# A two-layer transformer block and a third block on one core: norms between stages by token block, and an order of up panels

## The chip, the cores and the metric

One core of one Trainium2 chip runs the whole program. The metric is the device time of one execution in microseconds, the median of several runs; lower is better. Engines of the core: TensorE (PE; its weight loads are shown as PEld), VectorE (DVE), ScalarE (ACT), GpSimd (POOL), and SyncE (SP), which here only issues the DMA transfers.

## The reference

256 tokens of width 1024. Two layers (`hybrid_layer`) run one after the other, then a second block of another kind that this change touches only through its feed-forward. One layer is:

```python
shift1, scale1, gate1, shift2, scale2, gate2 = jnp.split(mod[:, None, :], 6, axis=-1)
h = rms_norm(x, norm1) * (1.0 + scale1) + shift1
proj = h @ w_in                       # 1816 columns: pool, queries, keys and values, gates
mix = jnp.concatenate([y_pool, y_nsa], axis=-1) @ w_out
x = x + gate1 * mix
h2 = rms_norm(x, norm2) * (1.0 + scale2) + shift2
ff = jnp.square(jax.nn.relu(h2 @ w_ff1)) @ w_ff2      # 1024 -> 4096 -> 1024
x = x + gate2 * ff
```

with `mod = silu(c) @ w_mod + b_mod` (6144 columns per layer) and `rms_norm(x, g) = x * rsqrt(mean(x * x) + eps) * g`.

## The kernel before

**Numbers.** Every float32 weight and activation is split in two parts of type fp32r: a rounded `hi` and a rest `lo`. A product is three matmuls, hi x hi, hi x lo and lo x hi (`mm3`, lines 433 to 437). `act2` holds `act_hi` and `act_lo` side by side, so in the up matmuls one instruction of 512 columns does hi x (hi and lo) for all 256 tokens (line 803) and one of 256 columns lo x hi (line 804).

**Weights** come in panels of 128 x 2048 (1 MB) through a ring of six. ScalarE copies a panel to `w_hi`, one of four slots (`split_hi`, line 425), VectorE writes the rest into the ring in place (`split_lo`, line 430), TensorE uses it and frees the slot (`pe_used`). A layer has 44 panels: 8 for the input projections, 4 for the output projection (two pool, two attention: `L_POOL`, `L_ATT`), and 16 up and 16 down panels of the feed-forward (`L_FF` = 12 on).

**Modulation** (`mod`) is computed on VectorE: a unit of `w_mod`, 1 MB, is multiplied by silu(c) and summed (`dve_mod`, line 1196, two instructions per unit). In layer 0, units 8 to 19 are turns 0 to 11 of the attention stage; in layer 1, units 12 to 21 are turns 0 to 9. They are loaded into two buffers in turn by SyncE (`gate_mod` in `sp_layer`): a unit's load waits until the unit two before it is summed.

**Order of the work.** Each engine runs a list written out by hand, and engines wait for each other's semaphores. All queues are in order, so an instruction that waits holds up all that stand behind it on its engine.

**Out projection to feed-forward.** `pe_out` puts the tokens' quarters (block of 128 tokens, half of the columns) into banks 0 to 3. For each quarter VectorE multiplies by the gate row and adds to x (`dve_update`, lines 1215 and 1217); ScalarE squares and sums it (`act_stats`, line 946) and after two quarters has 1/rms of the token block (line 954). VectorE scales the block (`dve_scaled`, line 1224), TensorE transposes it into banks 4 to 7 (`pe_features`, line 585), and per 128 features VectorE (even ones, line 1233) and ScalarE (odd ones, line 981) apply scale and shift for all 256 tokens, ScalarE rounds to `act_hi` and VectorE subtracts (line 1242, `act_ready`). The first up panel (`up_head`, lines 785 and 786) takes the features as they come.

**Feed-forward** (`pe_ff`). Up and down panels take turns, each up one step ahead. Behind an up panel ScalarE and VectorE build the square of the relu and split it (`ff_hi`, line 1155, and `ff_lo`, line 1497, `ff_ready`); a down panel waits for it. The last down panel goes by quarters, so that quarter after quarter of x can be updated.

**Between the layers** the same norm is done, with nothing for TensorE to do beside it: `pe_features`, then `pe_head` of the next layer's first panel. After layer 1, x itself is transposed for the second block, without a norm.

Of the kernel before, what the change touches and what calls it, by code (L numbers as in the profile page):

```python
# [14 lines left out]
P = 128  # L15
# [82 lines left out]
def build(nc, a, out, layers=DEPTH):  # L98
# [8 lines left out]
    with ctx:  # L107
# [141 lines left out]
        hb = [arena[:, y_at + i * T:y_at + (i + 1) * T] for i in range(6)]  # L249
        ybuf = [area(2 * T, 2, T) for _ in range(3)]  # L250
# [115 lines left out]
        def sp_layer(sp, l, ahead):  # L366
# [25 lines left out]
            gate_mod(9)  # L392
            load(sp, m, 14)
            load(sp, m, 15)
            gate_mod(10)
            gate_mod(11)
# [163 lines left out]

        def pe_out(pe, l, m, k, steps=(0, 8)):
# [26 lines left out]

        def pe_gate_row(pe, l, late, h, o):
# [7 lines left out]
        def pe_layer(pe, l, ahead):  # L597
            m = 11 * l

            def arrive(kc):  # L600
                pe.wait_ge(act_ready, 16 * l + max(kc + 1, 2))
# [164 lines left out]
            pe_used(pe, pe_out(pe, l, m, L_ATT + 1, (4, 8)))  # L766
            pe_features(pe, xn, y_ready, 8 * l + 4)
            pe_ff(pe, l, m, lambda kc: pe.wait_ge(act_ready, 16 * l + KC + kc + 1), 16 * l, L_FF)
            if ahead:
                pe_features(pe, xn, y_ready, 8 * l + 8)  # L770
            else:
                pe_features(pe, x, x_ready, 8 * l + 4)

        def pe_ff(pe, l, m, arrive, j0, k0, second=False):


            def up_head(mm, k, jn):

                pe.wait_ge(lo_done, 4 * mm + k + 1)
                wh, wl = w_hi[slot(k)], w_lo(mm, k)  # L780
                for kc in range(KC):
                    arrive(kc)
                    for c in range(2):
                        s = kc * 256 + c * P
                        nc.tensor.matmul(bank[c][:, :], wh[:, s:s + P], act2[:, kc, :, :], start=kc == 0, stop=False, skip_group_check=True)  # L785
                        last = nc.tensor.matmul(bank[c][:, 0:T], wl[:, s:s + P], act_hi[:, kc, :], start=False, stop=kc == KC - 1,
                                                skip_group_check=True)
                        if c == 0 and kc == KC - 1:
                            last.then_inc(ff_full, 1)
                pe_used(pe, last)  # L790
# [457 lines left out]
        def dve_layer(dve, l, link, ahead):  # L1248
# [76 lines left out]
            if l == 0:  # L1325
                split_lo(dve, m, 2)
# [1168 lines left out]
```

## Time and profile before

| | us |
|---|---|
| median of 3 runs | 1243.28 (1242.53 to 1245.27) |
| the profiled execution | 1243.92 |
| its span, first to last instruction | 1242.1 |
| TensorE busy | 1158.9 |
| VectorE busy | 916.0 |
| ScalarE busy | 622.1 |
| mean granted TensorE clock | 0.981 of full speed |

Matmuls are pipelined: a duration in the profile is longer than the time to the start of the next, so the pace is read from the starts. An entry in square brackets at the end of a timeline row is the time that the engine was idle before the instruction, and what released it.

### The profile page before, as it was taken

The page shows a single profiled execution, that of the slowest core. Times are in us where ns is not written, and L with a number is a line of the kernel's source. Part 1 is how long each engine was busy: PE and PEld are TensorE (multiplying, and loading weights), DVE is VectorE, ACT ScalarE, POOL GpSimd, SP SyncE. Part 2 cuts the span into 40 slices and gives each one's busy share as a digit, 9 for nine tenths or more (in the row PEclk, how much of TensorE's full clock was granted, in tenths as well). Part 3 has the DMA queues.
Part 4 walks back from the last instruction along what each step waited for, and adds up shares of the span by engine and source line. Part 5 has one row for each costly group of instructions (what it writes and reads, how often), then busy time and mean ns, then how long its engine had stood idle before and what let it go on. Part 6 is the DMA issues. An engine that isn't in the chain of part 4 may idle for free.

```text
span 1242.1 us, 18002 instructions
## 1 busy us (share of the span) xinstructions
PE 1158.9 (93%) x7130; PEld 1012.3 (81%) x7130; DVE 916.0 (74%) x1192; ACT 622.1 (50%) x851; POOL 58.5 (5%) x61
## 2 busy tenths in 40 slices
PE   1999979999979998999999998999889998999996
PEld 1978858888869787888888997888779997888885
DVE  6889789888767978856567369887984858656555
ACT  3763254444455525544444434568995634444441
POOL 1016000000000430000000000000000000000000
PEclk9999979999989999999999999999999999999998
DMA  9935557868756336555555533346864564555540
GB/s 380 379 128 214 201 188 277 307 244 315 265 205 237 136 103 249 200 177 199 185 186 195 176 135 131 104 154 218 288 223 136 177 231 168 170 177 196 188 150 34
DMA packets 44054, 249.27 MB, mean 201 GB/s; under 512 B 4352, under 2 KB 12672, under 8 KB 15952
## 3 DMA queue, kind: packets, MB, share of 16 engines
q1 hardware_dynamic: 43568, 246.19, 55.1%
q0 software_dynamic: 416, 2.11, 0.4%
q8 instruction: 49, 0.80, 0.3%
q14 instruction: 21, 0.17, 0.0%
HBM read 247.17 MB, written 1.11 MB: 200 GB/s over the span
## 4 chain that ended last, share of the span: by engine, by line
PE 77%; DVE 11%; ACT 5%; DMA 3%; issue 2%; SPq 0%; POOL 0%; DVEq 0%; ACTq 0%; POOLq 0%
PE bank L435 15%; PE bank L436 15%; PE bank L437 15%; PE bank L803 14%; PE bank L804 7%; PE bank L882 2%; DMA raw<-in_panels 2%; DVE ring_w L430 2%; DVE arena L2126 2%; PE bank L923 1%; ACT mixf L1947 1%; PE bank L785 1%; ACT mixf L1948 1%; PE bank L1739 1%; DMA arena<-in_modw 1%
## 5 line engine op out<-in xcount | busy, mean ns | idle before, releaser
L430 DVE TENSOR_TENSOR ring_w<-raw,w_hi 128x2048 fp32r<-128x2048 f32 x170 | 390.5, 2301 | 151.3 <-ACT w_hi L425 150.9
L425 ACT ACTIVATE w_hi<-raw 128x2048 fp32r<-128x2048 f32 x170 | 324.3, 1911 | 159.3 <-PE bank L437 144.6
L803 PE MATMUL bank<-act,w_hi 128*128 128x512 f32 x736 | 262.2, 399 | 0.2 <-DVE act L2263 0.2
L435 PE MATMUL bank<-act,w_hi 128*128 128x256 f32 x792 | 231.9, 293 | 3.6 <-ACT arena L1980 2.0
L436 PE MATMUL bank<-act,w_hi 128*128 128x256 f32 x792 | 226.0, 285 | 0.0
L437 PE MATMUL bank<-act,ring_w 128*128 128x256 f32 x792 | 225.9, 285 | 0.0
L804 PE MATMUL bank<-act,ring_w 128*128 128x256 f32 x736 | 206.6, 281 | 0.0
L803 PEld LDWEIGHTS bank<-act,w_hi 128*128 128x128 f32 x736 | 138.5, 188 | 34.4 <-issue 0.6
L435 PEld LDWEIGHTS bank<-act,w_hi 128*128 128x128 f32 x792 | 153.9, 194 | 12.2 <-issue 9.5
L436 PEld LDWEIGHTS bank<-act,w_hi 128*128 128x128 f32 x792 | 153.9, 194 | 0.1
L437 PEld LDWEIGHTS bank<-act,ring_w 128*128 128x128 f32 x792 | 153.8, 194 | 0.0
L435 PE MATMUL bank<-w_hi,ff_hi 128*128 128x512 f32 x384 | 149.9, 390 | 0.0
L436 PE MATMUL bank<-ring_w,ff_hi 128*128 128x512 f32 x384 | 149.9, 390 | 0.0
L437 PE MATMUL bank<-w_hi,ff_lo 128*128 128x512 f32 x384 | 149.4, 389 | 0.0
L804 PEld LDWEIGHTS bank<-act,ring_w 128*128 128x128 f32 x736 | 139.2, 189 | 1.6
L1148 ACT ACTIVATE arena<-bank 128x256 f32<-128x256 f32 x96 | 36.8, 385 | 160.9 <-PE bank L804 151.5
L1196 DVE CUSTOM_DVE_ANT_0 arena<-arena,crow 128x1024 f32<-128x1024 f32 x88 | 105.9, 1243 | 12.3 <-DMA arena<-in_modw 11.9
L1490 DVE TENSOR_TENSOR arena<-bank,arena 128x256 f32<-128x256 f32 x96 | 39.8, 421 | 64.6 <-ACT arena L1148 64.5
L435 PEld LDWEIGHTS bank<-w_hi,ff_hi 128*128 128x128 f32 x384 | 72.1, 188 | 15.9
L437 PEld LDWEIGHTS bank<-w_hi,ff_lo 128*128 128x128 f32 x384 | 72.1, 188 | 15.4
L436 PEld LDWEIGHTS bank<-ring_w,ff_hi 128*128 128x128 f32 x384 | 72.1, 188 | 13.3
L2126 DVE SCALAR_TENSOR_TENSOR arena<-arena 128x256 f32<-128x256 f32 x96 | 39.1, 479 | 9.7 <-ACT arena L1897 9.7
(349 smaller groups left out, 1652.9 us busy)
## 6 DMA issues: line engine op xcount, KB each, us to landing
raw<-in_panels SPq DMA_DIRECT2D x170, 1024.0 KB, 4.9
arena<-in_modw SPq DMA_DIRECT2D x44, 1024.0 KB, 7.2
mixf<-dscr SPq DMA_DIRECT2D x8, 512.0 KB, 4.9
arena<-dscr SPq DMA_DIRECT2D x8, 512.0 KB, 4.9
mixf<-in_modw SPq DMA_DIRECT2D x2, 1024.0 KB, 16.0
act_flat<-in_modw SPq DMA_DIRECT2D x2, 1024.0 KB, 20.0
mixf<-dscr SPq DMA_DIRECT2D x8, 256.0 KB, 5.9
arena<-dscr SPq DMA_DIRECT2D x8, 256.0 KB, 6.2
```

The source lines that it names most:

```text
L425: nc.scalar.activation(w_hi[slot(k)][:, :], w_raw(m, k), ACT.Copy).then_inc(hi_done, 1)
L430: nc.vector.tensor_tensor(w_lo(m, k), w_raw(m, k), w_hi[slot(k)][:, :].bitcast(F32), ALU.subtract).then_inc(lo_done, 1)
L435: nc.tensor.matmul(o, wh, xh, start=start, stop=False, skip_group_check=skip)
L436: nc.tensor.matmul(o, wh, xl, start=False, stop=False, skip_group_check=skip)
L437: return nc.tensor.matmul(o, wl, xh, start=False, stop=stop, skip_group_check=skip)
L803: nc.tensor.matmul(bank[4 + c][:, :], wh[:, s:s + P], act2[:, kc, :, :], start=kc == 0, stop=False)
L804: last = nc.tensor.matmul(bank[4 + c][:, 0:T], wl[:, s:s + P], act_hi[:, kc, :], start=False, stop=kc == KC - 1)
L882: mm = lambda o, w, x, first=False, last=False: nc.tensor.matmul(o, w, x, start=first, stop=last, skip_group_check=True)
L1148: nc.scalar.activation(fr[par][:, c * T:(c + 1) * T], up_bank(at, c, final)[:, T:2 * T], ACT.Copy).then_inc(ff_cross, 1)
L1196: last = nc.vector.tensor_tensor_reduce(o, o, crow[:, :], 1.0, 0.0, ALU.mult, ALU.add, sums[:, col + b:col + b + 1])
L1490: nc.vector.tensor_tensor(fr[par][:, c * T:(c + 1) * T], up_bank(at, c, final)[:, 0:T], fr[par][:, c * T:(c + 1) * T], ALU.add).then_inc(f ...
L2126: ins = nc.vector.scalar_tensor_tensor(xb[:, b, :], src, w, xb[:, b, :], ALU.mult, ALU.add)
```

## The change

Four edits. (1) The norm before the feed-forward and the norm between the layers go by two blocks of 128 tokens: ScalarE now scales a block, TensorE transposes it into banks 6 and 7, VectorE and ScalarE take four features each, and rounding and subtraction go by four features (512 columns) at a time. (2) The first two up panels of layers 0 and 1 run per token block: first panel on block 0, half of the second panel on block 0, the transposes of block 1, the other half, then both panels on block 1. (3) In layers 0 and 1 the last two down panels run by quarters. (4) The modulation sums stand one place or more earlier in VectorE's list, and their loads ahead of panels 14 and 15 in SyncE's. Besides, `up` issues a column half's eight wide matmuls and then its eight narrow ones, in all three feed-forwards.

```diff
+        def block_feature(kc):
+            return bank[6 + kc % 2][:, kc // 2 * P:(kc // 2 + 1) * P]
...
+            gate_mod(10)
+            gate_mod(11)
...
+        def pe_quarter(m, k, xh, xl, final, n):
+            wh, wl = w_hi[slot(k)], w_lo(m, k)
+            tt, h = n // 2, n % 2
+            for kk in range(2):
+                ts, s = slice(kk * T + tt * P, kk * T + (tt + 1) * P), slice(kk * D + 512 * h, kk * D + 512 * (h + 1))
+                last = mm3(bank[n][:, :], xh[:, ts], xl[:, ts], wh[:, s], wl[:, s], False, final and kk == 1, skip=True)
+            return last
...
+        def pe_block_features(pe, q, tt):
+            pe.wait_ge(y_ready, 4 * q + 2 * tt + 2)
+            for kc in (0, 2, 4, 6, 1, 3, 5, 7):
+                last = nc.tensor.transpose(block_feature(kc), xn[:, tt, kc * P:(kc + 1) * P], ident)
+                if kc >= 6:
+                    last.then_inc(xt_full, 1)
...
-                pe.wait_ge(act_ready, 16 * l + max(kc + 1, 2))
+                pe.wait_ge(act_ready, 16 * l + (6 + 2 * (kc // 4) if l else max(kc + 1, 2)))
...
-            pe_used(pe, pe_out(pe, l, m, L_ATT + 1, (4, 8)))
-            pe_features(pe, xn, y_ready, 8 * l + 4)
-            pe_ff(pe, l, m, lambda kc: pe.wait_ge(act_ready, 16 * l + KC + kc + 1), 16 * l, L_FF)
+            pe_out(pe, l, m, L_ATT + 1, (4, 6))
+            pe_block_features(pe, 2 * l + 1, 0)
+            pe_used(pe, pe_out(pe, l, m, L_ATT + 1, (6, 8)))
+            first, second = bank[0:2], bank[4:6]
+            pe_up_block(pe, l, m, L_FF, first, 0, range(KC))
+            pe_up_block(pe, l, m, L_FF + 1, second, 0, range(4))
+            pe_block_features(pe, 2 * l + 1, 1)
+            pe_up_block(pe, l, m, L_FF + 1, second, 0, range(4, KC))
+            pe_up_rest(pe, l, m, L_FF, first)
+            pe_up_rest(pe, l, m, L_FF + 1, second)
+            pe_ff(pe, l, m, None, 16 * l, L_FF)
             if ahead:
-                pe_features(pe, xn, y_ready, 8 * l + 8)
+                pe_block_features(pe, 2 * l + 2, 0)
+                pe_block_features(pe, 2 * l + 2, 1)
...
+        def pe_up_one(m, k, o, c, kc, tt):
+            wh, wl = w_hi[slot(k)], w_lo(m, k)
+            s, ts = kc * 256 + c * P, slice(tt * P, (tt + 1) * P)
+            both = o[c][:, :].rearrange("p (b t) -> p b t", b=2)[:, :, ts]
+            nc.tensor.matmul(both, wh[:, s:s + P], act2[:, kc, :, ts], start=kc == 0, stop=False, skip_group_check=True)
+            return nc.tensor.matmul(o[c][:, ts], wl[:, s:s + P], act_hi[:, kc, ts], start=False, stop=kc == KC - 1, skip_group_check=True)
+        def pe_up_block(pe, l, m, k, o, tt, kcs):
+            pe.wait_ge(lo_done, 4 * m + k + 1)
+            for kc in kcs:
+                pe.wait_ge(act_ready, 16 * l + KC + 4 * tt + 2 + 2 * (kc // 4))
+                for c in range(2):
+                    pe_up_one(m, k, o, c, kc, tt)
+        def pe_up_rest(pe, l, m, k, o):
+            for c in range(2):
+                for kc in range(KC):
+                    pe.wait_ge(act_ready, 16 * l + KC + 6 + 2 * (kc // 4))
+                    last = pe_up_one(m, k, o, c, kc, 1)
+                if c == 0:
+                    last.then_inc(ff_full, 1)
+            pe_used(pe, last)
...
                         nc.tensor.matmul(bank[4 + c][:, :], wh[:, s:s + P], act2[:, kc, :, :], start=kc == 0, stop=False)
+                    for kc in range(KC):
+                        s = kc * 256 + c * P
                         last = nc.tensor.matmul(bank[4 + c][:, 0:T], wl[:, s:s + P], act_hi[:, kc, :], start=False, stop=kc == KC - 1)
...
+                a = (e, k0 + 2, ff_hi[:, 0, :], ff_lo[:, 0, :], False)
+                b = (e, k0 + 3, ff_hi[:, 1, :], ff_lo[:, 1, :], True)
+                pe.wait_ge(ff_ready, 2 + j0 + FF_STEPS - 1)
+                pe.wait_ge(lo_done, 4 * e + k0 + 3)
+                for n in (0, 1, 2):
+                    pe_quarter(*a, n)
+                pe.wait_ge(ff_ready, 2 + j0 + FF_STEPS)
+                pe.wait_ge(lo_done, 4 * e + k0 + 4)
+                pe_quarter(*b, 0).then_inc(rows_done, 1)
+                pe_quarter(*b, 1).then_inc(rows_done, 1)
+                pe_used(pe, pe_quarter(*a, 3))
+                pe_quarter(*b, 2).then_inc(rows_done, 1)
+                pe_used(pe, pe_quarter(*b, 3))
...
+        def act_scaled(act, q, tt):
+            act.wait_ge(rs_done, 2 * q + tt + 1)
+            for h in range(2):
+                cols = slice(512 * h, 512 * (h + 1))
+                nc.scalar.activation(xn[:, tt, cols], x[:, tt, cols], ACT.Copy, scale=rs[:, tt:tt + 1]).then_inc(y_ready, 1)
+        def act_block(act, q, tt, g0, shift):
+            act.wait_ge(gcol_ready, q + 1)
+            act.wait_ge(xt_full, 4 * q + 2 * tt + 2)
+            if tt:
+                act.wait_ge(act_ready, 8 * q + 4)
+            for j in range(2):
+                for kc in (4 * j + 1, 4 * j + 3):
+                    last = nc.scalar.activation(hn[:, kc, :], block_feature(kc), ACT.Identity, bias=modc[:, shift + kc:shift + kc + 1],
+                                                scale=gcol[:, g0 + kc:g0 + kc + 1])
+                last.then_inc(h_done, 1)
+                act.wait_ge(t_done, 4 * q + 2 * tt + j + 1)
+                act.wait_ge(h_done, 4 * q + 2 * tt + j + 1)
+                nc.scalar.activation(act_hi[:, 4 * j:4 * j + 4, tt * P:(tt + 1) * P], hn[:, 4 * j:4 * j + 4, :], ACT.Copy).then_inc(act_his, 2)
...
-            for n in range(3):
-                act_stats(act, 2 * l + 1, n)
+            q = 2 * l + 1
+            act_stats(act, q, 0)
+            act_stats(act, q, 1)
+            act_scaled(act, q, 0)
+            act_block(act, q, 0, KC, 24)
+            act_stats(act, q, 2)
+            act_stats(act, q, 3)
+            act_scaled(act, q, 1)
+            act_block(act, q, 1, KC, 24)
             split_hi(act, m, 14)
-            act_stats(act, 2 * l + 1, 3)
-            act_norm(act, l, 2 * l + 1, 24, KC)
             act_ff(act, l, m, L_FF, 16 * l)
...
+                q = 2 * l + 2
+                for tt in range(TT):
+                    act_stats(act, q, 2 * tt)
+                    act_stats(act, q, 2 * tt + 1)
+                    act_scaled(act, q, tt)
+                    act_block(act, q, tt, 0, 0)
...
+        def dve_block(dve, q, tt, g0, shift):
+            dve.wait_ge(gcol_ready, q + 1)
+            dve.wait_ge(xt_full, 4 * q + 2 * tt + 1)
+            for kc in (0, 2, 4, 6):
+                last = nc.vector.tensor_scalar(hn[:, kc, :], block_feature(kc), gcol[:, g0 + kc:g0 + kc + 1], modc[:, shift + kc:shift + kc + 1],
+                                               ALU.mult, ALU.add)
+                if kc % 4:
+                    last.then_inc(t_done, 1)
+            for j in range(2):
+                v, ts = slice(4 * j, 4 * j + 4), slice(tt * P, (tt + 1) * P)
+                dve.wait_ge(act_his, 8 * q + 4 * tt + 2 * j + 2)
+                nc.vector.tensor_tensor(act_lo[:, v, ts], hn[:, v, :], act_hi[:, v, ts].bitcast(F32), ALU.subtract).then_inc(act_ready, 2)
...
+            mod(3)
...
             mixed(1)
+            mod(8)
             for g in range(4):
                 dve.wait_ge(pool_his, 4 * l + g // 2 * 2 + 2)
@@ -1417,15 +1520,15 @@
                 if g % 2:
                     last.then_inc(gfree[g // 2], 1)
             weigh(4)
+            mod(9)
             weigh(5)
             split_lo(dve, m, 11)
             weigh(6)
-            mod(7)
+            mod(10)
             mixed(2)
             weigh(7)
+            mod(11)
             mixed(3)
...
+            split_lo(dve, m, 13)
             update(0)
-            mod(10)
-            update(1)
-            mod(11)
             dve_modc(dve, modc_ready, 4 * l + 3, 24, lc[:, LC_BM + 8:LC_BM + 24], MOD_PANELS * l + (22 if l else 20))
             nc.vector.scalar_tensor_tensor(gcol[:, KC:2 * KC], modc[:, 32:40], 1.0, lc[:, LC_N2:LC_N2 + KC], ALU.add, ALU.mult).then_inc(gcol_ready, 1)
+            update(1)
             update(2)
-            dve_scaled(dve, 2 * l + 1, 0)
+            dve_block(dve, 2 * l + 1, 0, KC, 24)
             update(3)
-            dve_scaled(dve, 2 * l + 1, 1)
-            dve_norm(dve, 2 * l + 1, KC, 24)
-            split_lo(dve, m, 13)
+            dve_block(dve, 2 * l + 1, 1, KC, 24)
             split_lo(dve, m, 14)
...
-                    dve_scaled(dve, 2 * l + 2, n - 2)
+                    dve_block(dve, 2 * l + 2, n - 2, 0, 0)
+            if ahead:
+                split_lo(dve, m + 11, 2)
```

The first `mod(3)` line stands between the compression and `rotated(0)`; further down, the `mod(3)` to `mod(6)` of before become `mod(4)` to `mod(7)` in their places.

## Rows read from the trace of the kernel before

**Rows 1.** The page: busy us (share of the span) of each engine, xinstructions

```profile
PE 1158.9 (93%) x7130; PEld 1012.3 (81%) x7130; DVE 916.0 (74%) x1192; ACT 622.1 (50%) x851; POOL 58.5 (5%) x61
```

**Rows 2.** Timeline of TensorE, layer 1, projection to feed-forward: start, duration, engine, line, op

```profile
482.96 1.03 PE L585 MATMUL bank<-cst,arena 128*128 128x128 f32 x8
...
488.72 0.77 PE L785 MATMUL bank<-act,w_hi 128*128 128x512 f32 x1 [1.14 <-DVE act L1242]
...
495.81 0.40 PE L803 MATMUL bank<-act,w_hi 128*128 128x512 f32 x1
...
501.45 0.40 PE L435 MATMUL bank<-w_hi,ff_hi 128*128 128x512 f32 x1
...
506.92 0.39 PE L803 MATMUL bank<-act,w_hi 128*128 128x512 f32 x1
```

**Rows 3.** Timeline of TensorE, streams of 256 columns (layer 1) and of 60 (layer 0)

```profile
365.77 0.28 PE L435 MATMUL bank<-act,w_hi 128*128 128x256 f32 x1
...
371.88 0.28 PE L435 MATMUL bank<-act,w_hi 128*128 128x256 f32 x1
...
62.08 0.28 PE L435 MATMUL bank<-ff_hi,w_hi 128*128 128x60 f32 x1
...
63.08 0.28 PE L435 MATMUL bank<-ff_hi,w_hi 128*128 128x60 f32 x1
```

**Rows 4.** Timelines of VectorE and TensorE, layer 0, rotation and pool copies

```profile
68.21 0.69 DVE L1271 TENSOR_TENSOR arena<-bank,cst 128x512 f32<-128x512 f32 x1 [3.33 <-PE bank L613]
...
119.42 1.22 DVE L1196 CUSTOM_DVE_ANT_0 arena<-arena,crow 128x1024 f32<-128x1024 f32 x1
...
123.06 0.42 DVE L1322 TENSOR_TENSOR mix_lo<-bank,mix_hi 128x256 fp32r<-128x256 f32 x1 [1.28 <-ACT mix_hi L1066]
...
124.12 1.74 DVE L1415 SCALAR_TENSOR_TENSOR mix_lo<-bank,lc,mix_hi 128x256 fp32r<-128x256 f32 x4 [0.63 <-ACT mix_hi L1118]
...
125.05 0.48 PE L919 MATMUL bank<-vca,act_flat 32*128 32x130 f32 x2 [0.54 <-DVE mix_lo L1415]
```

**Rows 5.** Timelines of VectorE and TensorE, layer 0, projection to feed-forward

```profile
153.53 1.23 DVE L1196 CUSTOM_DVE_ANT_0 arena<-arena,crow 128x1024 f32<-128x1024 f32 x1 [2.41 <-DMA arena<-in_modw]
...
155.39 0.39 PE L437 MATMUL bank<-w_hi,mix_lo 128*128 128x512 f32 x1
...
168.58 0.76 PE L785 MATMUL bank<-act,w_hi 128*128 128x512 f32 x1 [0.72 <-DVE act L1242]
...
182.52 0.40 PE L435 MATMUL bank<-w_hi,ff_hi 128*128 128x512 f32 x1
```

**Rows 6.** Timelines of ScalarE and VectorE, layer 1: rounding of panel 13, first ff_lo

```profile
472.33 1.92 ACT L425 ACTIVATE w_hi<-raw 128x2048 fp32r<-128x2048 f32 x1 [2.44 <-PE bank L437]
...
500.44 0.69 DVE L1497 TENSOR_TENSOR ff_lo<-arena,ff_hi 128x512 fp32r<-128x512 f32 x1
```

**Rows 7.** Timeline of ScalarE: root of a block (layer 1), scaled copies (start of the program)

```profile
479.82 0.63 ACT L946 ACTIVATE arena<-x 128x512 f32<-128x512 f32 x1 [0.28 <-DVE x L1217]
...
480.91 0.20 ACT L954 ACTIVATE rs<-sq_log 128x1 f32<-128x1 f32 x1
...
9.85 1.34 ACT L2382 ACTIVATE arena<-x,rs 128x512 f32<-128x512 f32 x2
```

**Rows 8.** Timelines of VectorE and TensorE, layer 0 to layer 1

```profile
346.69 2.29 DVE L430 TENSOR_TENSOR ring_w<-raw,w_hi 128x2048 fp32r<-128x2048 f32 x1
...
348.89 0.68 DVE L1215 TENSOR_TENSOR arena<-bank,arena 128x512 f32<-128x512 f32 x1
...
350.22 0.68 DVE L1215 TENSOR_TENSOR arena<-bank,arena 128x512 f32<-128x512 f32 x1
...
349.51 0.39 PE L437 MATMUL bank<-w_hi,ff_lo 128*128 128x512 f32 x1
...
360.10 0.55 PE L435 MATMUL bank<-act,w_hi 128*128 128x256 f32 x1 [1.05 <-DVE act L1242]
...
365.36 0.33 PE L435 MATMUL bank<-act,w_hi 128*128 128x256 f32 x1
```

More of the change, by code:

```diff
@@ L771, in pe_layer @@
             else:
                 pe_features(pe, x, x_ready, 8 * l + 4)
-        def pe_ff(pe, l, m, arrive, j0, k0, second=False):
[L777 to L790, printed above, removed]
+        def pe_up_one(m, k, o, c, kc, tt):
[4 more added lines that the diff above has]
+            return nc.tensor.matmul(o[c][:, ts], wl[:, s:s + P], act_hi[:, kc, ts], start=False, stop=kc == KC - 1, skip_group_check=True)
@@ L814, in pe_ff @@
                 up(m, k0, j0, 0, arrive)
-            else:
-                up_head(m, k0, j0)
-            up(m, k0 + 1, j0 + 1, 1, waits=second)
+                up(m, k0 + 1, j0 + 1, 1)
             down(m, k0 + 2, j0, 0, True, False)
@@ L832, in pe_ff @@
             up(e, k0 + 1, j0 + FF_STEPS - 1, 1)
-            down(e, k0 + 2, j0 + FF_STEPS - 2, 0, False, False)
-            down(e, k0 + 3, j0 + FF_STEPS - 1, 1, False, True)
+            if second:
+                down(e, k0 + 2, j0 + FF_STEPS - 2, 0, False, False)
+                down(e, k0 + 3, j0 + FF_STEPS - 1, 1, False, True)
+            else:
+                a = (e, k0 + 2, ff_hi[:, 0, :], ff_lo[:, 0, :], False)
[11 more added lines that the diff above has]
+                pe_used(pe, pe_quarter(*b, 3))
         pair_of = lambda ap: ap.rearrange("p (b s) -> p b s", b=2)
@@ L1217, in dve_update @@
             nc.vector.tensor_tensor(x[:, tt, cols], x[:, tt, cols], xn[:, tt, cols], ALU.add).then_inc(x_ready, 1)
-        def dve_scaled(dve, q, tt):
-            dve.wait_ge(rs_done, 2 * q + tt + 1)
-            for h in range(2):
-                cols = slice(512 * h, 512 * (h + 1))
-                nc.vector.tensor_scalar(xn[:, tt, cols], x[:, tt, cols], rs[:, tt:tt + 1], None, ALU.mult).then_inc(y_ready, 1)
+        def dve_block(dve, q, tt, g0, shift):
[10 more added lines that the diff above has]
+                nc.vector.tensor_tensor(act_lo[:, v, ts], hn[:, v, :], act_hi[:, v, ts].bitcast(F32), ALU.subtract).then_inc(act_ready, 2)
         def dve_norm(dve, q, g0, shift):
@@ L1395, in dve_layer @@
             stack(1)
-            mod(3)
+            mod(4)
             split_lo(dve, m, 8)
-            mod(4)
+            mod(5)
             split_lo(dve, m, 9)
@@ L1405, in dve_layer @@
                 dve_modc(dve, modc_ready, 4 * l + 2, 16, lc[:, LC_BM:LC_BM + 8], 12)
-            mod(5)
+            mod(6)
             weigh(2)
@@ L1409, in dve_layer @@
             mixed(0)
-            mod(6)
+            mod(7)
             mixed(1)
+            mod(8)
             for g in range(4):
@@ L1422, in dve_layer @@
             weigh(6)
-            mod(7)
+            mod(10)
             mixed(2)
             weigh(7)
+            mod(11)
             mixed(3)
-            mod(8)
-            mod(9)
             def update(n):
```

11 lines of the change are left out of this document (4 added, 7 removed).

## The prediction

> **What bounds the kernel now.** I read the page first: TensorE is busy for 93% of the span [rows 1]. So a change pays where TensorE stands still or runs slowly, and costs where it gets more matmuls. Next the timeline of TensorE alone, where the start-to-start step counts (the durations overlap). In the feed-forward an up panel (32 matmuls) takes 495.81 to 501.45, 5.64 us, and a down panel (24) 501.45 to 506.92, 5.47 us [rows 2]; all panels of the three feed-forwards that I measured repeat these two numbers within 0.03 us, without a gap. The engine is short of work at the stage borders, and these I read last, engine by engine: out projection to feed-forward in both layers (part 3), and layer 0 to layer 1 (part 4).
>
> **1. The up panel's new order.** `up` now issues 8 matmuls of 512 columns and then 8 of 256, where it alternated; 44 panels go through it (14 in each layer, 16 in the last feed-forward; 2 per layer now go through the block helpers). All are on TensorE's path. Alternating, a pair costs 5.64/16 = 0.3525 us. A stream of 512 columns alone costs 5.47/24 = 0.228 [rows 2], one of 256 alone (371.88-365.77)/51 = 0.120 [rows 3]: 0.348 a pair, 0.08 us less per panel, 44 times: **-3.5 us**. No row shows grouped weights of both kinds, so the bounds are 0 (nothing is saved by the order) and -5.3 (half as much again). I take -3.5, since both streams are rows.
> The Trainium skill, page "TensorE: Matmul & The Clock Gate", section "Back-to-back issue gap", gives the gap of a single matmul as N/2.4 + 2.5 ns, 109 and 216 ns here, whatever stands beside it; by it the order changes nothing. The rows are above it by 11 ns each, and the pair by 28 ns.
>
> **2. Modulation sums moved forward.** One sum is two multiply-reduces of 1.22 us that overlap a little, 2.3 us in all [rows 4]. The one now ahead of the rotation lies in an idle stretch of VectorE of 3.3 us [rows 4]: nothing, unless its unit lands over 1 us late. The one between the first two pairs of weighings takes the place of another: nothing. But `mod(8)` now stands between `mixed(1)` and the four pool copies. VectorE is free there only from about 123.4 to 124.1, then the copies start, and TensorE waits for them (idle 0.54 with the copy as releaser) [rows 4]. The sum ends at 123.4+2.3 = 125.7, 1.6 us after the copies began before; TensorE gets its banks that much later. Both layers: **+3.2 us**. Bounds: +2.4 (a shorter start) to +5 (the sum's own DMA late). The sums behind weighings 4, 6 and 7 lie where VectorE waits for TensorE or ScalarE anyway, and delay at most its last mix copy, which TensorE needs only with the fourth matmul group of the attention part: nothing. On SP, units 18 and 19 now go ahead of panels 14 and 15. A unit is issued when the sum two before it is done, and these sums now end before the panel whose slot the load of panel 14 needs: no queue delay; if they came late, panel 14 would, and with it a split that has some 20 us in hand.
>
> **3. Out projection to feed-forward.** The length counts from the end of the projection to the first down panel. Before: layer 1 482.96 to 501.45, 18.5 us [rows 2]; layer 0 155.62 to 182.52, 26.9 us, longer because VectorE waits 2.4 us for a sum's DMA and then does sums before it updates x [rows 5].
> After, in layer 1's times: panel 13's rounding ends on ScalarE at 474.2 [rows 6]; VectorE subtracts it (2.2), updates 0 and 1 (1.33 each [rows 8]), so x's second quarter is there at 479.5. ScalarE needs 1.3 for the root and 1.35 for the two scaled copies that it takes over [rows 7]: xn at 482.2. TensorE has done all but 6 matmuls at 481.6, waits 0.6, transposes (1.0 [rows 2]), does the 6 and is at 484.7. Behind the transposes a block needs: 1.1 for them, ScalarE's two 128-column pieces and one 512-wide copy (1.45, estimated from the 1.35 for two such copies), VectorE's subtraction 0.7 [rows 6]: first half at 3.3 us, second half at 4.6 us. So the first up panel starts at 485.6, 3.1 us earlier than 488.72.
> But the block matmuls cost more. A pair is 256+128 columns. The 256 costs 0.12; for 128 no row is at hand, but 60 columns cost (63.08-62.08)/9 = 0.111 [rows 3], so a narrow matmul is not under that: 0.23 a pair, twice, against 0.3525. Bounds for the 128: 0.06 (half of the 256) to 0.21 (as slow as at half clock). I take 0.11. The two panels have 64 such pairs, 14.7 us, against 11.3.
> The last update of x is queued behind block 0's subtraction (487), the stats of block 1 behind that: x at 488.2, xn at 490.9, block 1's first half at 494.3, its second at 495.7. TensorE has done its three portions of block 0 and one of block 1 at 493.8, waits about 0.5 twice, ends the first panel's second column half at 498.4 and the second panel at 502.0. Then what is late is the first ff half: from the first panel's end to its `ff_lo` 495.81 to 501.13, 5.3 us [rows 2, 6], was hidden behind a whole up panel of 5.64; now behind 3.6. The first down panel starts at 498.4+5.4 = 503.8.
> So the length is 20.8 in both layers (layer 0's sums no longer decide): layer 1 **+2.4**, layer 0 **-6.1**. Bounds: 17.4 (narrow matmuls at 0.06, no ff wait) and 25 a layer.
>
> **4. Layer 0 to layer 1.** TensorE ends at 349.74 and starts layer 1 at 360.10 [rows 8]. The quarters bring x's rows earlier, but VectorE is busy until 346.69 anyway; it gains the 2.2 us of the weight subtraction that stood there [rows 8]. Three updates end at 350.75, the root is ready at 350.75 too, scaled copies 352.1, transposes, block 0 done on VectorE at 356.7. Only then comes the last update (358.1), root 359.4, scaled copies 360.8, transposes at half clock (2 us), first half of block 1 at about 365.1; and the layer's head needs both blocks. No matmul fills this. Before, the four updates ran one behind the other. **+5.0 us**. Bounds +2.5 and +7. Half the clock for the head is paid in both (25 matmuls from 360.10 to 365.36 take 0.21 each against 0.12 [rows 3, 8]), 2.2 us, give or take 1.
>
> **5. Before the second block** the last quarter ends at the same time, and its update is the last before the head: 0. Bounds -0.7 and +1.
>
> **Sum:** -3.5 + 3.2 + 2.4 - 6.1 + 5.0 = **+1.0 us**, on the profiled execution's 1243.92 (span 1242.1 and 1.8 around it). This execution is 0.6 above the median of the runs, 1243.28; the forecast is that median plus 1.0, **1244.3 us**.
>
> **Rivals.**
> A. *The pipelining pays in full, 0.29.* TensorE's block matmuls run at 0.09, the ff half comes in time behind the second panel, and the order of `up` gives 5.3. For it: the first down panel's wait in my sum is only 1.8 us and rests on four estimated pieces. Against it: the 60-column row. Layers -1.8 each, `up` -1.8 more: 1.0-5.4 = -4.4, **1238.9 us**.
> B. *Slower: the order of `up` gives nothing, 0.21.* Place: 44 panels. Price: my -3.5 goes. It decides as soon as a grouped pair costs 0.3525. Everything else stands at +4.5: **1247.8 us**. For it: a pair's excess over its two streams is 0.005 us, so small that it may belong to something else in the panel than the order. That is also where the page's rule leads.
> C. *Slower: TensorE's clock falls at the block border, 0.08.* Its waits of 0.6 to 1.8 us there follow one another; before, a 2.5 us idle had it at half speed for the head in layer 1. Up to 2.5 us per layer: **1249 us**.
> D. *The blocks do nothing, 0.04:* the head waits as before and the narrow matmuls' 3.4 us are pure cost. Layer 1 18.5+3.4, and layer 0 the same, 5.0 below its 26.9: with the other parts +3.1, **1246.4 us**.
> My own forecast: 0.38.
>
> **How the numbers follow.** A measurement here tells 0.2% (2.5 us) from no change. Faster: A 0.27 and 0.03 of my own forecast's spread, 0.30. Slower: B 0.17, C and D 0.12, 0.04 of my own, 0.33. Same: 0.37. Since the sides nearly balance, the likeliest case's own range is 1241 to 1247.5; the range to hold 8 in 10 is 1238.5 to 1249.5.
>
> **What would show it.** Right: the granted clock still falls between the layers, and layer 1's first panel starts some 15 us after layer 0's last down matmul (10.4 before); TensorE idles about 2 us before the pool copies' consumer in both layers; up panels take 5.56; the first down panel waits for `ff_lo` and starts about 21 us after the projection's end in both layers. Wrong: 128-column matmuls at 0.06 or at 0.2; up panels at 5.64; a head of layer 1 before 362; the pool copies not moved.

## The result and the profile after

The change makes the kernel slower: 1255.69 us median of 8 runs (1248.42 to 1267.90) against 1243.75 (1242.53 to 1246.08); the ratio of comparable runs is 1.0072, 95% interval 1.0046 to 1.0099. Forecast were 1244.3 us and a range to 1249.5. The ratios leave out a run that is over 1.5% above the fastest of its kernel: here the profiled execution, the slowest of the eight, 1267.90 us, span 1266.1. Its page:

```profile
span 1266.1 us, 18288 instructions
...
PE 1177.9 (93%) x7258; PEld 1034.0 (82%) x7258; DVE 912.6 (72%) x1180; ACT 633.0 (50%) x863; POOL 58.6 (5%) x61
...
PEclk9999799999969988999999999899999999899999
```

TensorE's share is the same 93% as before [rows 1], so the page's first line says nothing. PEclk (the granted clock in 40 equal slices, in tenths of full speed) has a 7 in its fifth digit and 8s in its fifteenth and sixteenth, where before has 9s. I then took the start of each stage's first matmul from TensorE's timeline; the table has the lengths in us of the profiled executions, those of the experiments (below) beside them. "Order" is the new order in the up panels, "sums" the moved modulation sums.

| stage on TensorE | before | after | sums | sums, ninth behind the copies | the same + order | + mid blocks | + border blocks, quarters | all, ninth sum behind |
|---|---|---|---|---|---|---|---|---|
| first matmul stream to layer 0's projection | 103.9 | 113.3 | 105.7 | 104.2 | 104.5 | 104.7 | 103.9 | 104.8 |
| layer 0: projection's start to first down panel | 40.6 | 35.5 | 32.9 | 32.4 | 33.4 | 35.5 | 33.2 | 35.5 |
| last two down panels of layer 0 to layer 1's head | 21.3 | 28.1 | 21.3 | 21.3 | 21.3 | 21.3 | 27.4 | 27.2 |
| layer 1: head to projection | 109.1 | 118.6 | 110.3 | 108.6 | 108.2 | 108.6 | 108.3 | 109.4 |
| layer 1: projection's start to first down panel | 32.2 | 35.7 | 33.0 | 33.4 | 33.1 | 35.5 | 33.2 | 37.3 |
| the same feed-forward from there | 156.3 | 155.4 | 156.3 | 156.3 | 155.3 | 157.0 | 155.3 | 155.4 |

Before to after the spans differ by 24.0 us: +9.4 and +9.5 in the two attention stages, +6.8 between the layers, +3.5 in layer 1's border, -5.2 in layer 0's, -0.9, -0.9 and -1.1 in the feed-forwards; 2.8 are the program's start (0.5) and the second block (2.3), which the change does not touch. Most of the 2.3 is a fall of the clock too: behind a wait of 1.83 us, from 932.4 to 936.0 at a granted clock of 0.54, where before has the same wait of 1.83 us and no fall. The two big terms are not in my sum. What they are is seen in the stretch behind the pool copies. First after, by windows (stretch, its length, busy us and count of PE, PEld, DVE, ACT and POOL, granted clock PEclk, DMA share, GB/s):

```profile
127.22:144.66 17.44, 17.44 (x57) 13.91 (x57) 10.55 (x20) 0.61 (x1) 0.00 (x0) 0.51 0.36 122
151.81:187.27 35.46, 31.25 (x206) 27.75 (x205) 23.95 (x36) 22.31 (x42) 0.00 (x0) 1.00 0.53 191
342.65:370.72 28.07, 15.01 (x67) 12.00 (x65) 16.53 (x29) 14.88 (x33) 0.61 (x1) 0.73 0.55 203
...
464.68:482.00 17.32, 17.32 (x57) 13.79 (x57) 9.74 (x19) 0.61 (x1) 0.00 (x0) 0.51 0.00 1
489.30:525.02 35.72, 31.24 (x207) 27.74 (x205) 22.53 (x32) 22.30 (x42) 0.59 (x1) 1.00 0.56 201
```

The same windows of before:

```profile
125.05:134.73 9.68, 9.68 (x57) 7.73 (x57) 6.49 (x14) 2.19 (x2) 0.00 (x0) 1.00 0.09 36
141.89:182.52 40.63, 31.76 (x143) 26.32 (x141) 32.90 (x52) 17.98 (x36) 0.00 (x0) 0.83 0.61 236
338.83:360.10 21.27, 14.13 (x66) 11.27 (x65) 17.59 (x28) 11.03 (x23) 0.61 (x1) 0.89 0.71 266
469.23:501.45 32.22, 28.59 (x142) 24.00 (x141) 28.24 (x44) 18.00 (x36) 0.59 (x1) 0.95 0.64 243
```

The 57 matmuls from the first one behind the pool copies took 9.7 us at full clock before and take 17.4 us after, TensorE busy all the time, at a granted clock of 0.51: the level of 1.2 GHz. That is 7.8 us, in each layer. The wait right ahead of the fall stands in TensorE's timeline of after, both layers:

```profile
127.22 0.80 PE L979 MATMUL bank<-vca,act_flat 32*128 32x130 f32 x2 [2.11 <-DVE mix_lo L1518]
...
464.68 0.48 PE L979 MATMUL bank<-vca,act_flat 32*128 32x130 f32 x2 [2.11 <-DVE mix_lo L1518]
```

and VectorE's timeline of after, layer 0, has the reason of the wait:

```profile
123.67 0.42 DVE L1423 TENSOR_TENSOR mix_lo<-bank,mix_hi 128x256 fp32r<-128x256 f32 x1 [1.29 <-ACT mix_hi L1150]
124.00 1.22 DVE L1289 CUSTOM_DVE_ANT_0 arena<-arena,crow 128x1024 f32<-128x1024 f32 x1
...
125.15 1.22 DVE L1289 CUSTOM_DVE_ANT_0 arena<-arena,crow 128x1024 f32<-128x1024 f32 x1
...
126.29 1.66 DVE L1518 SCALAR_TENSOR_TENSOR mix_lo<-bank,lc,mix_hi 128x256 fp32r<-128x256 f32 x4
```

The ninth sum starts at 124.00 and the copies behind it only at 126.29, and TensorE stands 2.11 us instead of 0.54 [rows 4]: 1.57 us a layer, as forecast (1.6). The fall of the clock behind it was not.

The up panels went as forecast. TensorE's timeline of after, one panel of layer 1 in four groups of 8:

```profile
530.60 1.98 PE L848 MATMUL bank<-act,w_hi 128*128 128x512 f32 x8
532.41 1.12 PE L851 MATMUL bank<-act,ring_w 128*128 128x256 f32 x8
533.36 2.00 PE L848 MATMUL bank<-act,w_hi 128*128 128x512 f32 x8
535.20 1.12 PE L851 MATMUL bank<-act,ring_w 128*128 128x256 f32 x8
536.15 0.40 PE L440 MATMUL bank<-w_hi,ff_hi 128*128 128x512 f32 x1
```

530.60 to 536.15 is 5.55 us against 5.64 [rows 2]; a wide matmul steps 0.226, a narrow one 0.119.

### The profile page after: what moved, and what is told of

Same layout as the page of the kernel before. It is cut to its first block, busy times and chain, and to the rows that moved or that the text cites. A ratio compares the mean times of both kernels' runs of the same rounds, so it can differ in the third digit from the quotient of the medians.

```text
span 1266.1 us, 18288 instructions
## 1 busy us (share of the span) xinstructions
PE 1177.9 (93%) x7258; PEld 1034.0 (82%) x7258; DVE 912.6 (72%) x1180; ACT 633.0 (50%) x863; POOL 58.6 (5%) x61
## 3 DMA queue, kind: packets, MB, share of 16 engines
q0 software_dynamic: 416, 2.11, 0.5%
## 4 chain that ended last, share of the span: by engine, by line
PE 53%; DVE 10%; ACT 5%; issue 2%; POOL 0%; DVEq 0%; ACTq 0%
PE bank L440 11%; PE bank L441 11%; PE bank L442 11%; PE bank L848 9%; PE bank L851 5%; DVE ring_w L435 2%; DVE arena L2227 2%; PE bank L942 1%; ACT mixf L2048 1%; PE bank L983 1%; ACT w_hi L430 1%; ACT mixf L2049 1%; PE bank L1840 1%; PE bank L1894 1%; PE bank L813 0%
## 5 line engine op out<-in xcount | busy, mean ns | idle before, releaser
L435 DVE TENSOR_TENSOR ring_w<-raw,w_hi 128x2048 fp32r<-128x2048 f32 x170 | 390.5, 2300 | 157.5 <-ACT w_hi L430 157.0
L442 PE MATMUL bank<-act,ring_w 128*128 128x256 f32 x792 | 226.1, 285 | 0.0
L848 PE MATMUL bank<-act,w_hi 128*128 128x512 f32 x704 | 177.5, 395 | 0.6 <-DVE act L2364 0.6
L440 PEld LDWEIGHTS bank<-act,w_hi 128*128 128x128 f32 x792 | 154.2, 195 | 14.1 <-issue 11.6
L441 PEld LDWEIGHTS bank<-act,w_hi 128*128 128x128 f32 x792 | 154.2, 195 | 0.1
L442 PEld LDWEIGHTS bank<-act,ring_w 128*128 128x128 f32 x792 | 154.0, 194 | 0.0
L848 PEld LDWEIGHTS bank<-act,w_hi 128*128 128x128 f32 x704 | 130.5, 190 | 26.1 <-issue 0.8
L851 PEld LDWEIGHTS bank<-act,ring_w 128*128 128x128 f32 x704 | 96.9, 192 | 7.0
L851 PE MATMUL bank<-act,ring_w 128*128 128x256 f32 x704 | 99.0, 284 | 0.0
```

What stands on the lines that cost most here:

```text
L435: nc.vector.tensor_tensor(w_lo(m, k), w_raw(m, k), w_hi[slot(k)][:, :].bitcast(F32), ALU.subtract).then_inc(lo_done, 1)
L440: nc.tensor.matmul(o, wh, xh, start=start, stop=False, skip_group_check=skip)
L441: nc.tensor.matmul(o, wh, xl, start=False, stop=False, skip_group_check=skip)
L442: return nc.tensor.matmul(o, wl, xh, start=False, stop=stop, skip_group_check=skip)
L848: nc.tensor.matmul(bank[4 + c][:, :], wh[:, s:s + P], act2[:, kc, :, :], start=kc == 0, stop=False)
L851: last = nc.tensor.matmul(bank[4 + c][:, 0:T], wl[:, s:s + P], act_hi[:, kc, :], start=False, stop=kc == KC - 1)
```

## Experiments

The theory after these rows: the change's own work costs some 4 to 5 us net, and the clock's fall behind the pool copies 7.5 us in each layer and run in which it happens. The eight times of after lie in such steps, and so do their mean granted clocks: three at 1248.4 to 1249.4 (0.985), four at 1255.4 to 1257.2 (0.977 to 0.979), one at 1267.9 (0.968). The rivals: the loss comes from the border between the layers, or the clock falls for a reason of its own. Ratios are to before on the same chip; the interval stands behind. Medians of two kernels come in part from different chips, and their differences are good to about 1 us: before itself has medians of 1243.8, 1244.0 and 1245.6 on the three chips of these runs.

**The ninth sum behind the copies, the rest as after.**

```
             mixed(1)
-            mod(8)
             for g in range(4):   # the four pool copies
             ...
+            mod(8)
             weigh(4)
```

> After, with the ninth modulation sum (mod(8)) behind the four pool copies instead of ahead of them; nothing else. Theory 1 (clock): in the profiled run of after, TensorE stood 2.1 us for the pool copies in each layer and ran at half clock from there for 17 us, so the sum cost 1.6 us plus up to 7.8 us per layer. Then this kernel shows no half clock between 125 and 145 us nor in the same place of layer 1, the second pair of pool matmul groups takes its 9.7 us again, and the median is 1243 to 1247 us. Theory 2 (only the delay of 1.6 us a layer comes from the sum, the clock falls for another reason): 1252.5 us, half clock still there.

Measured 1248.48 us (7 runs, 1245.45 to 1252.76), ratio 1.0039 (1.0021 to 1.0058). The windows behind the copies, layers 0 and 1, and the two borders behind them:

```profile
125.50:135.20 9.70, 9.70 (x58) 7.75 (x58) 9.49 (x19) 2.19 (x2) 0.00 (x0) 1.00 0.58 194
452.93:462.70 9.77, 9.77 (x58) 7.82 (x58) 9.56 (x19) 2.17 (x2) 0.00 (x0) 1.00 0.09 34
333.19:360.42 27.23, 14.16 (x67) 11.29 (x65) 16.53 (x29) 14.88 (x33) 0.61 (x1) 0.76 0.56 209
469.77:507.07 37.30, 32.83 (x206) 29.30 (x204) 22.63 (x32) 22.29 (x42) 0.59 (x1) 0.95 0.53 192
```

The clock stays up, the 58 matmuls take 9.7 us again, and 7.2 us of the median go with one moved sum. By the ratios of the two kernels, 1.0072 and 1.0039, it is 4.1 us, and their intervals overlap; so the clock in the rows shows the effect here, and the pair of kernels below shows it in the times. No run reaches after's usual 1255. The median is 1.5 above my span of 1243 to 1247: the rest costs more than I had it.

**The sums alone, on before.** The edit is the part of the diff that moves `mod(...)` and `gate_mod(...)`.

> Before, with the modulation sums and the loads of their units moved as in the change; no other part. Theory 1 (clock): slower by the delay of 3.2 us and by 0 to 7.8 us per layer, different from run to run: 1247 to 1262 us, with TensorE at half clock behind the pool copies in at least one layer of the profile. Theory 2 (the delay alone): 1247.0 us in every run, no half clock there.

1242.87 us (11 runs), ratio 0.9998 (0.9972 to 1.0025): eight runs at 1239.1 to 1244.0 and three at 1251.6, 1255.9 and 1258.0, where before never exceeded 1248.4 in 24. In the profiled execution TensorE waits 2.11 us in both layers and the clock does not fall:

```profile
127.41:137.10 9.69, 9.69 (x58) 7.73 (x58) 8.59 (x18) 0.62 (x1) 0.00 (x0) 1.00 0.66 217
...
448.26:458.00 9.74, 9.74 (x58) 7.79 (x58) 8.64 (x18) 0.62 (x1) 0.00 (x0) 1.00 0.00 0
```

So a wait of 2.1 us may or may not be followed by the fall, and my demand that it show in this profile was a miss. So was the median: both theories had 1247 us or more. The table has what I had under-read: the sums alone shorten layer 0's border from 40.6 to 32.9 us.

**The same with the ninth sum behind the copies.**

```
             mixed(1)
             for g in range(4):   # the four pool copies
             ...
+            mod(8)
             weigh(4)
+            mod(9)
             weigh(5)
```

> Before, with the modulation sums and their loads moved as in the change, but the ninth sum (mod(8)) behind the pool copies; no other part. Theory 1 (clock): no wait of 2.1 us for the pool copies, so no half clock there in any run, and the runs lie close together; what the moved sums bring remains: with the ninth sum ahead of the copies layer 0's out projection to its first down panel took 32.9 us against 40.6 before. 1243.8 - 7.7 + about 1 in layer 0 and 1 in layer 1: 1238 us, no run above 1244. Theory 2 (the spread of 1239 to 1258 us has nothing to do with the place of this sum): the same median of 1243, and again some runs above 1250.

1237.73 us (7 runs, 1236.34 to 1242.50), ratio 0.9954 (0.9938 to 0.9970). No high runs, 5.1 us below the kernel with that one sum ahead, and the intervals of the two ratios lie apart. Moving the sums is worth 6.3 us, if the ninth keeps off the copies.

**The order of the up panels alone.**

```
                     for kc in range(KC):
                         ... wide matmul
+                    for kc in range(KC):
+                        s = kc * 256 + c * P
                         last = ... narrow matmul
```

> Before, with only the order of the matmuls in the up panels changed (8 wide, then 8 narrow). In after a panel takes 5.56 us instead of 5.64. If that is the order's doing: 44 x 0.08 = 3.5 us less, 1240.2 us, panels of 5.56 us. Rival (the shorter panel has another reason, or the clock gives the gain back): 1243.7 us.

1240.63 us (12 runs), ratio 0.9982 (0.9972 to 0.9992): -3.2 us, panels of 5.56. The gain is the order's.

**Order and sums together (ninth behind the copies).** No blocks, no quarters.

> The same, and the new order in the up panels (8 wide, then 8 narrow): no blocks, no quarters. If the two parts add: 3.5 us less than the kernel with the sums alone, 1234.5 us, better than before and after. If the gains cancel through the clock: 1238 us.

1235.40 us (6 runs), ratio 0.9925 (0.9912 to 0.9938). In medians the order gives -2.3 on top of the sums against -3.2 alone, in ratios -3.6 against -2.2: the parts add as far as these runs can tell. This kernel is the base of the rest, since it leaves out exactly the blocks and the quarters.

**Base plus the blocks between projection and feed-forward.** Edit: the parts of the diff at `pe_block_features(pe, 2 * l + 1, ...)`, `pe_up_block`, `act_block` and `dve_block`.

> The same as the kernel with up order and moved sums, plus the blocks between out projection and feed-forward in both layers; norm between the layers and last down panels as in before. Theory: the blocks cost; layer 0's projection to first down panel took 35.5 us in every kernel with blocks and 32.9 with the sums moved and no blocks, layer 1's 35.5 to 37.3 against 32.2 to 33.0: +2.5 and +3 to +4.5, so 6 to 7 us more than without them, 1241 us. Rival (it is the sums that were kept from working by the blocks' wait on the layer's clock, the blocks themselves pay as my rival A had it): 1.8 us less per layer, 1231 us.

1240.75 us (12 runs), ratio 0.9977 (0.9965 to 0.9989): +5.35 us (6.5 by the ratios). Both borders take 35.5 us at full clock, against 33.4 and 33.1 at a granted clock of 0.90 without blocks. Rival A is out. In this execution the clock falls right behind layer 1's border, which costs the feed-forward 1.6 us (157.0 against 155.4); in the first experiment it fell inside that border, at 0.95 above, 37.3 against 35.5. These are 2 of the 8 block borders in the profiled executions of the four kernels that have them, and the waits ahead of them were short: 1.51 us here, 0.98 and 0.30 us there.

```profile
143.36:178.83 35.47, 31.28 (x207) 27.76 (x205) 24.20 (x36) 22.30 (x42) 0.00 (x0) 1.00 0.53 191
...
464.10:499.56 35.46, 31.26 (x206) 27.74 (x204) 22.54 (x32) 22.29 (x42) 0.59 (x1) 1.00 0.55 201
499.56:656.56 157.00, 157.00 (x792) 134.04 (x793) 99.77 (x95) 70.72 (x71) 0.00 (x0) 0.99 0.54 187
```

**Base plus the blocks between the layers, with quarters.** Edit: the parts of the diff at `2 * l + 2` and `pe_quarter`.

> The same as the kernel with up order and moved sums, plus the blocks between layer 0 and layer 1 and the last down panels by quarters; the norms inside the layers as in before. Theory: from layer 0's last two down panels to layer 1's first matmul 27.2 us instead of 21.3, and the rest unchanged: 5.9 us more than without them, 1240.5 us. Rival (the stretch is long only because the layer's clock had been pushed down by what came before it): 22 to 24 us, 1236 us.

1240.79 us (9 runs), ratio 0.9970 (0.9958 to 0.9982): +5.4 us (5.6 by the ratios), the stretch 27.4 us. The rival is out.

**After with the old norm between the layers, quarters kept.**

> After, with the norm between layer 0 and layer 1 done as in before (one block of 256 tokens, root scaled on VectorE, the weight subtraction ahead of the updates); quarters, mid norms and modulation sums stay as in after. In after, the stretch from layer 0's last down panels to layer 1's first matmul takes 28.1 us against 21.3 before. Theory: that is the two blocks' doing; 5 to 6.8 us less than after, about 1250 us, the stretch back at 21 us. Rival (the quarters or the clock make it long): 1255.7 us, stretch still 26 to 28 us.

1254.95 us (4 runs, 1253.54 to 1258.45), ratio 1.0101 (1.0086 to 1.0116). A miss: the median hardly moved, and the stretch took 23.8 us, not 21. With so few runs, in which the clock falls as it likes, the median can't show 4 us; in the profiled one it fell in layer 0 alone, at the same wait of 2.11 us in both layers:

```profile
127.25:145.00 17.75, 17.75 (x59) 14.06 (x59) 11.19 (x22) 0.61 (x1) 0.00 (x0) 0.52 0.36 120
...
459.86:469.50 9.64, 9.64 (x57) 7.73 (x57) 8.54 (x18) 0.62 (x1) 0.00 (x0) 1.00 0.01 2
```

The 23.8 us asked for a kernel of their own.

**Base plus the quarters alone.**

> The kernel with up order and moved sums (1235.4 us), plus only the last two down panels of the first two feed-forwards by quarters; norms as in before. The kernel that had the quarters under the old norm between the layers took 23.8 us from the last down panels to layer 1's first matmul, against 21.3: the slot of the last but one panel comes free later, ScalarE's rounding of layer 1's first panel and VectorE's subtraction wait for it, and the updates are queued behind that. Theory: 23.8 us again, +2.5 us, 1237.9 us. Rival (it was the half clock of that run, 13.7 us long): 21.3 us, 1235.4 us.

1237.81 us (5 runs), ratio 0.9940 (0.9925 to 0.9954), the stretch 23.8 us: +2.4 us in medians of different chips, 1.9 by the ratios, whose intervals overlap; the 2.5 us show in the stretch. VectorE's timeline between the layers:

```profile
338.18 0.17 DVE L1483 SCALAR_TENSOR_TENSOR gcol<-modc,lc 128x8 f32<-128x8 f32 x1
340.81 2.29 DVE L430 TENSOR_TENSOR ring_w<-raw,w_hi 128x2048 fp32r<-128x2048 f32 x1 [2.46 <-ACT w_hi L425]
343.01 0.68 DVE L1242 TENSOR_TENSOR arena<-bank,arena 128x512 f32<-128x512 f32 x1
```

The subtraction of layer 1's first panel waits 2.46 us for its rounding, as the slot comes free only with the quarter that the last but one panel now does late, and the updates are queued behind it. Before, it did not wait [rows 8]. The quarters bring x's rows earlier, and nothing takes them earlier.

**How long TensorE must stand.** First one of the ninth sum's two reduces ahead of the copies, then both the ninth and the tenth sum.

```
             mixed(1)
+            mod(8, 0)            # first half of the sum; in the other kernel: mod(8), mod(9)
             for g in range(4):
             ...
-            mod(8)
+            mod(8, 1)
```

> The kernel with up order and moved sums, where the ninth sum is split: its first multiply-reduce (1.22 us) ahead of the pool copies, the second behind them. TensorE's idle time there should be about 1.0 us (0.54 without a sum, 2.11 with a whole one). Theory (the clock falls only if TensorE stands long enough there): 0 to 1 us more than 1235.4 us, no half clock behind the pool copies in the profile and no run above 1243. Rival (any delay tips it in some runs): some runs 7 us above the others.

> The kernel with up order and moved sums, with the ninth and tenth sums both ahead of the pool copies; TensorE should stand some 4.4 us there in each layer. Theory: delay of 3.9 us a layer less the 1 us that the later sum cost, and half clock behind the pool copies in both layers in most runs, 7.5 us each: 1235.4 + 7 + 15 = 1257 us, few runs below 1250. Rival (the clock's fall there has nothing to do with the wait): 1242 us and the same share of high runs as without.

Half a sum: 1235.94 us (6 runs, 1234.71 to 1240.49), ratio 0.9932 (0.9915 to 0.9949). TensorE waits 0.96 us and the clock stays up. Its timeline, then the windows:

```profile
124.76 0.48 PE L921 MATMUL bank<-vca,act_flat 32*128 32x130 f32 x2 [0.96 <-DVE mix_lo L1419]
```

```profile
124.76:134.40 9.64, 9.64 (x57) 7.74 (x57) 9.40 (x19) 1.77 (x1) 0.00 (x0) 1.00 0.69 229
443.95:453.60 9.65, 9.65 (x57) 7.73 (x57) 9.41 (x19) 1.76 (x1) 0.00 (x0) 1.00 0.02 8
```

Two sums: 1259.64 us (4 runs, 1255.44 to 1262.32; 1257 expected), ratio 1.0124 (1.0105 to 1.0142), no run without the loss. The wait is longer than the expected 4.4 us. Timeline and windows of TensorE:

```profile
129.70 0.80 PE L921 MATMUL bank<-vca,act_flat 32*128 32x130 f32 x2 [5.42 <-DVE mix_lo L1420]
...
455.45 0.80 PE L921 MATMUL bank<-vca,act_flat 32*128 32x130 f32 x2 [5.27 <-DVE mix_lo L1420]
```

```profile
129.70:146.00 16.30, 16.30 (x84) 13.26 (x85) 9.66 (x19) 0.15 (x1) 0.00 (x0) 0.83 0.20 66
455.45:475.00 19.55, 19.55 (x72) 15.69 (x72) 7.47 (x15) 0.00 (x0) 0.00 (x0) 0.55 0.00 1
```

In the profiled executions, then: behind waits of 0.5 to 1.0 us in this place the clock never fell, behind 2.11 us in 3 of 6 (after twice, the kernel with the old norm between the layers once, the sums alone never), behind 5.3 us and more in both. The fall's length differs: against the kernel with half a sum ahead, layer 0 lost 2.5 us here (84 matmuls in 16.30 us for 13.84), layer 1 8.0 us (72 in 19.55 for 11.55).

**A version better than both.** Base, with two small parts of the change between the layers and without its blocks.

```
-                split_lo(dve, m + 11, 2)
             for n in range(4):
                 ... update
-                if ahead and n >= 2:
-                    dve_scaled(dve, 2 * l + 2, n - 2)
+                if ahead and n == 2:
+                    dve_scaled(dve, 2 * l + 2, 0)
+            if ahead:
+                split_lo(dve, m + 11, 2)
... ScalarE, behind its four stats:
+                act_scaled(act, 2 * l + 2, 1)
```

> The kernel with up order and moved sums, and between the layers two small parts of the change without its blocks: VectorE's subtraction of layer 1's first panel (2.3 us) stands behind the four updates instead of ahead of them, and ScalarE scales the second block (1.34 us for the two copies against 0.88 on VectorE), so that the subtraction runs beside it. From the last down panels to layer 1's first matmul 21.3 - 2.2 + 0.5 = 19.6 us, 1233.7 us in all. Rival (the updates wait for TensorE's last quarter anyway, or the later subtraction makes layer 1's head wait): 1235.4 us.

1234.28 us (5 runs, 1231.46 to 1234.94), ratio 0.9909 (0.9892 to 0.9925); the base's was 0.9925. The stretch takes 19.1 us (forecast 19.6):

```profile
331.38:350.44 19.06, 13.90 (x67) 10.92 (x65) 16.71 (x26) 12.37 (x25) 0.61 (x1) 0.93 0.68 251
```

The intervals of the two overlap; the 2.2 us show in the stretch.

## Why the prediction was wrong

The step that failed is part 2, the modulation sums: "TensorE gets its banks that much later. Both layers: **+3.2 us**. Bounds: +2.4 (a shorter start) to +5 (the sum's own DMA late)". The mechanism and the delay were right to 0.03 us; but a wait that grows from 0.5 to 2.1 us was priced at its own length. It also tips the clock, which costs the 57 matmuls behind it another 7.8 us where it happens. Delay and clock together are 7.2 us of after's median (4.1 by the ratios), and 5.1 with the sums alone. Rival C had the clock, but put it at the block borders, where the waits are shorter (the largest 1.5 us in after), for up to 2.5 us a layer. There it did come, in none of after's borders but in 2 of 8 in all, for 1.8 and 1.6 us. I did not ask the same of the wait that part 2 made. That the idle ahead of a stage without slack was 0.54 and the new one four times that stood in my own rows.

The other terms, by their measured sizes:

1. The up panels: -3.5 forecast; 5.56 us a panel, -3.2 us alone and -2.3 on top of the sums. Rival B is out. By the Trainium skill, page "TensorE: Matmul & The Clock Gate", section "Back-to-back issue gap", whose gap for a single matmul depends on its columns alone, the order should have changed nothing; the measurement decides.
2. The other sums: taken at nothing in the attention part, rightly. But what they bring stands in part 3.
3. Layer 0's border: -6.1 forecast, -5.2 measured (40.6 us at a granted clock of 0.83 before, 35.5 at 1.00 in after). The sign came from the sums, not from the blocks: with them moved and no block it is -7.2 to -8.2, and the blocks take 2.1 to 3.1 of that back. I had written that the sums "no longer decide" and left the blocks' cost in one number with it. Layer 1's border: +2.4 forecast, +3.5 measured in after, +3.2 in the kernel with these blocks alone. Of its pieces: TensorE's wait for the scaled copies 0.50 (0.6 forecast); 24 pairs of block matmuls 5.57 us, 0.232 a pair (0.23); the first down panel's wait for `ff_lo` 1.50 (1.8). What was off is block 1: its scaled copies end 0.3 us later than forecast, its transposes then stand another 0.3 us behind the 24 pairs on TensorE, and from them to the first half it takes 3.8 us, not 3.4. So that half comes 26.1 us behind the projection's start, not 25.1. TensorE's timeline of after, layer 1:

```profile
502.31 1.09 PE L609 MATMUL bank<-cst,arena 128*128 128x128 f32 x8 [0.50 <-ACT arena L1021]
...
505.99 0.36 PE L813 MATMUL bank<-act,w_hi 128*128 128x256 f32 x1 [1.20 <-DVE act L1325]
...
515.39 0.38 PE L813 MATMUL bank<-act,w_hi 128*128 128x256 f32 x1 [0.97 <-DVE act L1325]
...
525.02 0.50 PE L440 MATMUL bank<-w_hi,ff_hi 128*128 128x512 f32 x1 [1.50 <-DVE ff_lo L1598]
```

4. Layer 0 to layer 1: +5.0 forecast, +6.8 in after, +6.0 to +6.1 in the two other kernels with these blocks. The order of events is the forecast one; both halves of the chain are longer than their sums. VectorE's timeline of after:

```profile
350.50 0.69 DVE L1308 TENSOR_TENSOR arena<-bank,arena 128x512 f32<-128x512 f32 x1
...
357.20 1.36 DVE L1318 TENSOR_SCALAR arena<-bank,gcol,modc 128x128 f32<-128x128 f32 x4 [2.64 <-PE bank L609]
359.69 0.69 DVE L1325 TENSOR_TENSOR act<-arena,act 128x512 fp32r<-128x512 f32 x1 [1.13 <-ACT act L1037]
361.14 0.69 DVE L1325 TENSOR_TENSOR act<-arena,act 128x512 fp32r<-128x512 f32 x1 [0.75 <-ACT act L1037]
361.75 0.68 DVE L1308 TENSOR_TENSOR arena<-bank,arena 128x512 f32<-128x512 f32 x1
...
367.12 1.37 DVE L1318 TENSOR_SCALAR arena<-bank,gcol,modc 128x128 f32<-128x128 f32 x4 [3.96 <-PE bank L609]
```

The updates start 7.85 us behind the first of the last two down panels, as VectorE came free before (7.86 [rows 8]). Block 0 is done 11.25 us later (10.0 forecast), the head starts at 20.2 (18.4). VectorE waits 2.64, 1.13, 0.75 and 3.96 us in it: two blocks make two serial chains over three engines, and TensorE has no matmul to put beside either.
5. Before the second block: 0 forecast, 13.80 us before and after.

With the measured sizes, and no fall of the clock, my sum is -3.5 + 3.1 + 3.5 - 5.2 + 6.0 to 6.8 = +3.9 to +4.7, 1247 to 1248 us; the three lowest runs of after are 1248.4 to 1249.4. The forecast was 1244.3: some 3 to 4 us of its error are mis-sized terms, and the 8 from there to the median are one fall of the clock (7.8 in the rows). The parts measured one by one, -3.2 - 6.3 + 5.35 + 5.4 + 7.2, give +8.5 on the medians, of after's 11.9. By the ratios they are -2.2 - 5.7 + 6.5 + 5.6 + 4.1 = +8.3, of after's 9.0. So the 3.5 left over on the medians come mostly from after's times lying in steps, with the median on the upper one. Rival D, blocks as pure cost, had the right sign and too small a price.

What stays open: why the fall follows a wait of 2.1 us in some executions and not in others. In after it took five of eight runs (by their times), in the sums alone three of eleven. What TensorE did just ahead does not tell the places apart: in all six with a wait of 2.11 us it did 70 matmuls in the 10 us ahead of the wait, without a pause and at a granted clock of 1.00. Whether other work ahead of the wait shifts the odds, I did not try.

## What to carry to other kernels

Price a new wait of TensorE twice: by its length, and by the clock of what runs behind it, with a chance; two delays of 1.6 us took 4 to 7 us, and next to nothing once one 2.3 us operation of VectorE stood behind the urgent copies instead of ahead of them. Pipelining a norm in two blocks pays only where the other engines have work to put beside it; where each block is one chain over three engines, two blocks are two chains. And when one edit brings several parts, measure them alone: here two parts worth 8.6 us were hidden below two that cost 11 and one misplaced line that cost 7.

## What the hardware showed unexpectedly

- Ahead of the pool copies' matmuls the clock fell behind waits of 2.11 us in 3 of 6 places, never behind 0.96, always behind 5.3; once down, 57 matmuls that take 9.7 us took 17.4, with TensorE busy all the while.
- In other places the lengths differ. It fell inside a block border behind waits of 0.98 and 0.30 us, and behind one of 1.51 us, in 2 of 8 borders. In the border without blocks, where TensorE waits 2.49 us for the scaled block and 0.7 to 1.1 us more behind the transposes, it fell in all 18 places of the ten kernels that have it, for 3 to 7 us. So no length of a single wait tells the fall in these traces.
- A matmul of 128 columns costs 0.112 us by estimate (a pair of 0.232 less 0.120 for the 256 of [rows 3]), hardly less than one of 256: halving the tokens of a narrow matmul gains next to nothing. The Trainium skill, page "TensorE: Matmul & The Clock Gate", section "Back-to-back issue gap", gives 56 ns for a single one and about 81 in a stream with weight loads; the trace is above both.
- Alternating matmuls of 512 and 256 columns cost 0.005 us a pair more than the same in groups of eight.
